# Query and key norms made before the softmax steps, in a one-core MLA, pooling and PEER decoder step

## The reference, cut to what matters

```python
def rmsnorm(x, g):
    y = x * lax.rsqrt(jnp.mean(x * x, axis=-1, keepdims=True) + EPS)
    return y * g
...
q = (cq @ w_uq).reshape(b, t, N_HEADS, QK_NOPE_DIM + QK_ROPE_DIM)
qn = rmsnorm(q[..., :QK_NOPE_DIM], g_qn_nope)
qr = apply_rope(rmsnorm(q[..., QK_NOPE_DIM:], g_qn_rope), cos, sin)
kn = rmsnorm(einsum('...c,chd->...hd', lat, w_uk), g_kn_nope)
s = (einsum('bqhd,bkhd->bhqk', qn, kn) + einsum('bqhr,bkr->bhqk', qr, kr)) * ATTN_SCALE
s = where(k_pos <= q_pos, s, -inf)
p = softmax(s, axis=-1)
ctx = einsum('bhqk,bkc->bqhc', p, lat);  o = einsum('bqhc,chv->bqhv', ctx, w_uv)
```

## Time and profile before

| | us |
|---|---|
| median of 3 runs | 3472.05 (3469.83 to 3478.44) |
| the profiled execution | 3475.48 |
| its span in the trace | 3473.7 |
| attention of tile 0, first score matmul to output projection | 220.68 to 249.08 |
| the same of tile 1 | 297.51 to 329.75 |
| the same of tile 2 | 363.59 to 399.79 |
| PEER gathers | from 478.01 to the end |

### The profile page before, as it was taken

The page is one execution under the profiler, slowest core; times in us unless marked ns, Lnnn a source line. Parts: engine busy times, 40 slices in busy tenths (PEclk is TensorE's granted clock), DMA queues, the critical chain, the costliest instruction groups (busy, mean ns, idle before and its releaser), DMA issues.

```text
span 3473.7 us, 39504 instructions
## 1 busy us (share of the span) xinstructions
PE 2771.9 (80%) x11255; PEld 1237.1 (36%) x11255; DVE 2278.1 (66%) x6380; ACT 1041.5 (30%) x4438; POOL 1221.4 (35%) x1077
## 2 busy tenths in 40 slices
PE   6888889969889957988989769979875676566765
PEld 2344554424434413434434234434331232112321
DVE  2544568887777856777777575777776545565455
ACT  1222224424334412433434324434321111111111
POOL 0000014434333423433434334433444444544343
PEclk8979999989999979999989989999988777777777
DMA  8740059999999989999999999999999999999998
GB/s 329 277 175 34 13 199 408 405 363 404 365 378 413 405 341 371 415 398 406 411 391 403 415 365 405 413 409 410 397 400 410 421 421 408 420 394 369 422 419 358
DMA packets 201396, 1264.74 MB, mean 364 GB/s; under 512 B 23689, under 2 KB 44730, under 8 KB 61393
## 3 DMA queue, kind: packets, MB, share of 16 engines
q0 software_dynamic: 150784, 1091.03, 77.0%
q1 hardware_dynamic: 50393, 171.18, 12.9%
HBM read 1258.79 MB, written 3.79 MB: 363 GB/s over the span
## 4 chain that ended last, share of the span: by engine, by line
PE 41%; DMA 29%; DVE 15%; issue 8%; ACT 3%; POOL 3%; SPq 2%; DVEq 0%; POOLq 0%; ACTq 0%; PEldq 0%
PE bank L1144 14%; DMA ring<-in_uv,work 11%; DMA big<-in_uv,work 7%; PE bank L882 7%; DMA mod_mix<-in_uv,work 7%; PE bank L994 5%; DVE ring L2020 2%; PE bank L899 2%; DMA ring<-in_w_ada 2%; PE bank L828 2%; PE bank L696 1%; ACT work L1473 1%; POOL ring L1512 1%; PE bank L634 1%; PE bank L726 1%
## 5 line engine op out<-in xcount | busy, mean ns | idle before, releaser
L1144 PE MATMUL bank<-ring,work 128*64 128x512 f32 (+1 forms) x2080 | 898.0, 706 | 278.6 <-ACT work L1473 278.4
L1512 POOL DMA_INDIRECT ring<-in_uv,work x520 | 605.2, 1164 | 943.6 <-PE bank L1144 818.4
L2020 DVE CUSTOM_DVE_ANT_0 ring<-ring,mod_smp 128x1024 f32<-128x1024 f32 x512 | 621.9, 1224 | 271.8 <-DMA ring<-in_uv,work 264.7
L1461 ACT ACTIVATE work<-work 128x2 f32<-128x2 f32 x520 | 105.1, 202 | 1494.6 <-DVE work L2020 1494.0
L1512 POOL DMA_INDIRECT big<-in_uv,work x260 | 311.2, 1197 | 686.2 <-PE bank L1144 365.0
L882 PE MATMUL bank<-big 128*128 128x512 f32 x1024 | 515.5, 627 | 0.0
L1144 PE MATMUL bank<-big,work 128*64 128x512 f32 (+1 forms) x1040 | 313.8, 722 | 156.1 <-ACT work L1473 156.0
L1144 PEld LDWEIGHTS bank<-ring,work 128*64 128x64 f32 (+1 forms) x2080 | 207.9, 152 | 625.8 <-ACT work L1473 389.9
L2020 DVE CUSTOM_DVE_ANT_0 big<-big,mod_smp 128x1024 f32<-128x1024 f32 x256 | 309.5, 1224 | 132.4 <-DMA big<-in_uv,work 128.4
L1144 PE MATMUL bank<-work 128*64 128x512 f32 (+1 forms) x520 | 291.2, 688 | 96.2 <-ACT work L1473 96.0
L1473 ACT ACTIVATE work<-small,work 128x64 f32<-128x64 f32 (+1 forms) x1040 | 303.2, 339 | 144.6 <-DVE work L2030 139.0
(11 more groups left out here) (299 smaller groups left out, 3427.7 us busy)
## 6 DMA issues: line engine op xcount, KB each, us to landing
big<-in_wk SPq DMA_DIRECT2D x48, 1152.0 KB, 10.4
ring<-in_w_ada SPq DMA_DIRECT2D x64, 768.0 KB
work<-in_cache_mla SPq DMA_DIRECT2D x104, 160.0 KB, 5.3
ring<-in_uv,work POOLq DMA_INDIRECT x520, 11.8
big<-in_uv,work POOLq DMA_INDIRECT x260, 11.9
ring<-in_w_mla_out SPq DMA_DIRECT2D x1, 4096.0 KB, 14.1
big<-in_w_mla_out SPq DMA_DIRECT2D x4, 1024.0 KB, 11.6
mod_smp<-in_cache_mla SPq DMA_DIRECT2D x24, 160.0 KB, 10.6
```

Source lines behind the costliest of these rows:

```text
L1144: last = mm(out, diag[:, t % 2, j, 0:min(m, HALF)], s[:, D + half * 512:D + (half + 1) * 512], start=(k == 0 and (n < S0 or j == 0)), stop ...
L1461: act.activation(acts[:, t % 2 * GRP:(t % 2 + 1) * GRP], dots[:, t % 2 * GRP:(t % 2 + 1) * GRP], ACT.Gelu)\
L1512: pool.indirect_dma_start(slot[g % SLOTS], None, T["uv"].rearrange("l e d -> (l e) d"), bass.IndirectOffsetOnAxis(index[:, k * GRP + j:k * ...
L2020: dve.tensor_tensor_reduce(u, u, hb, 1.0, 0.0, ALU.mult, ALU.add, dots[:, at:at + 1]).then_inc(sem("dots_set"), 1)
```

## The change

Two edits. First, in `attend` of tiles 0 and 1 the parts 0, 1 and 2 of the next tile's `heads_norm` are executed ahead of the first row max, and the parts 3, 4 and 5 after heads 0, 2 and 4 in place of the parts 0 to 5 after heads 0 to 5. In tile 2 the parts stay where they were. Second, the multiplication of the plain queries by `gqn` (L1621) is kept for the sample tile alone. For the prompt tiles the weight is applied by ACT when it copies the transposed queries out of PSUM: there a query dimension is a partition, so `gqn` becomes a scale operand with one number per partition. That column, `q_gain`, is made once, by multiplying the identity with `gqn` and summing each row.

```diff
+        HEAD_PARTS, HEAD_STEP = (3, 3, 0), (2, 2, 1)
+        q_gain = tiny[:, 50:51]
...
                 for b in range(2):
-                    copy(qnT[:, b * 512:(b + 1) * 512], pb[(4 if i == 1 else 6) + b][:, :])
+                    w.done(act.activation(qnT[:, b * 512:(b + 1) * 512], pb[(4 if i == 1 else 6) + b][:, :], ACT.Copy, scale=q_gain))
...
                 elif part == 3:
                     d(tt(q3[:, :, 0:NOPE], q3[:, :, 0:NOPE], heads(8, NOPE), ALU.mult))
-                    d(tt(q3[:, :, 0:NOPE], q3[:, :, 0:NOPE], over_heads(gqn, NOPE), ALU.mult))
+                    if t == NT:
+                        d(tt(q3[:, :, 0:NOPE], q3[:, :, 0:NOPE], over_heads(gqn, NOPE), ALU.mult))
...
+                if t < NT - 1:
+                    for part in range(HEAD_PARTS[t]):
+                        heads_norm(t + 2, part)
                 row_max(0)
                 row_max(1)
...
                     if h < 6:
                         if t < NT - 1:
-                            heads_norm(t + 2, h)
+                            if h % HEAD_STEP[t] == 0 and HEAD_PARTS[t] + h // HEAD_STEP[t] < 6:
+                                heads_norm(t + 2, HEAD_PARTS[t] + h // HEAD_STEP[t])
...
             d(ts(gqr, gqr, SCALE, None, ALU.mult))
+            d(stt(sq[:, 0:NOPE], ident, 1.0, gqn, ALU.mult, ALU.mult, accum_out=q_gain))
```

## The result

| | before | after |
|---|---|---|
| median of the runs, us | 3474.32 (3466.25 to 3479.07, 8 runs) | 3454.59 (3449.88 to 3462.52, 8 runs) |
| ratio after / before | | 0.995, 95% interval 0.9938 to 0.9962 |
| span of the profiled execution | 3473.7 | 3450.9 |

The interval of the ratio is a gain of 13 to 22 us; the medians differ by 19.7. The forecast was a gain of 17.6 us, to 3454.5.

A forecast was written before the change was run, and what follows sets the result against it. The prediction took DVE to set the length of attentions 0 and 1. Gains of 8.6, 7.8 and 1.2 us in attentions 0, 1 and 2 sum to 17.6, taking 3472.05 to 3454.5 us; range 3446 to 3464.

The forecast's parts named there:

- DVE sets the length: Attentions 0 and 1: DVE decides their length, busy 24.4 of 28.4 and 27.1 of 32.2 us, after idling before each.
- The moved parts are hidden: Parts 0 to 2, 9.1 us per tile, fit DVE's idle time, ending 26 and 6 us before the first row max.
- Attention 0, 8.6 us: Attention 0 gets 8.6 us shorter, taken between 10.0 at full clock and 6.9 at the lower; projection change counted zero.
- The walk with two clocks: Attention 0's sequence rebuilt from row durations: projection starts 10.0 us earlier at full clock, 6.9 at the lower one.
- Attention 1, 7.8 us: Attention 1 gets 7.8 us shorter, taken between 9.7 at full clock and 4.5 at the lower.
- Attention 2, 1.2 us: Attention 2 loses only L1621, 1.26 us; taken as 1.2 us shorter, between 0 and 2.
- No price for the edits: Scaled copies on ACT and making `q_gain` on DVE cost nothing; upper ends 1.2 us per tile and 0.5 us.
- The output weights' cover of 4.6 us: Output weights land at 234.5, first projection wants them at 239 to 240: 4.6 us of cover left from 14.6.
- Full clock: Rival: PE keeps 2.4 GHz through both attentions, gain 23 us, 3449 us; chance 0.13.
- Low clock: Rival: lower clock comes as early as before and lasts into the projection, gain 11 to 12.6 us, 3460; chance 0.17.
- Given back: Rival: the PEER stage keeps 8 us or more of the 17.6 gained, 3463 to 3470 us; chance 0.09.
- Slower: Rival: PEER stage's granted clock drops from 0.93 to 0.91, costing 29 us, 3484 us; chance 0.04.

The follow-up runs named there:

- e2: Changed kernel with the norm weight put back on DVE, so only the parts of the norms move; 3453.97 us, ratio 0.9941.
- e3: Changed kernel with all six parts of the norms ahead of the first row max in tiles 0 and 1; 3444.97 us, ratio 0.9918.
- e4: Changed kernel plus matmuls that nothing reads on PE where it waits for part 4, in attentions 0 and 1; 3454.66 us, ratio 0.9948.
- e1: Changed kernel with all parts put back after heads 0 to 5, so only the scaled copies stay; 3468.31 us, ratio 0.9988.
- e5: e3 with the output weights loaded in two 2 MB halves, each with its own semaphore; 3440.96 us, ratio 0.9897.
- e6: e5 with parts 4 and 5 of the norms in tile 2 moved behind the last softmax step; 3435.83 us, ratio 0.988.
- e7: Changed kernel with parts 3, 4 and 5 after heads 0, 1 and 2 instead of 0, 2 and 4; 3452.47 us, ratio 0.9932.

## Why the prediction was right

- *DVE sets the length.* Right, and shown: e2 and e3 take DVE work out of attentions 0 and 1 and change nothing else, and these shrink.
- *The moved parts are hidden.* Right: 9.0 us from 183.7 and again from 271.45, the second 6.04 us before the first row max; the forecast was 9.1 and 6.
- *Attention 0, 8.6 us.* It measured 7.94, and 0.7 to 0.85 more in the projection behind it, for which I had counted nothing. That the two together meet 8.6 is luck: the term was 0.7 too high, the projection's 0.7 too low. The walk with two clocks gave 10.0 and 6.9. The fall came at part 4's gap, as expected: about 12 us after the first scores, where it came about 8 us after them before.
- *Attention 1, 7.8 us.* This term was mis-sized: 6.3. I put it near the full-clock end (9.7), though the gap was forecast and is followed by the low clock to the end of the attention. e4, without the gap, takes 9.0. The projection behind it was 0.5 shorter, which I had not counted either.
- *Attention 2, 1.2 us.* It measured 1.0 in one profile and 2.5 in the other; e2, where L1621 stays, took 35.85, e1, where it goes, 35.87. The single instruction can't be read from this attention, whose length depends on when the clock falls.
- *The sum.* 17.6 forecast, 16.4 measured up to the first gather. The rest of the difference of the medians, 19.7, lies within the spread of the runs. That the median after, 3454.59, is the forecast to 0.1 us is luck: the kernel before has a median of 3474.32 over eight runs, 2.3 us above the 3472.05 of the three runs that the forecast started from, and 17.6 from that is 3456.7.
- *No price for the edits.* Right within the path. The scaled copy of 128x512 takes 0.69 us, the unscaled one 0.60, so two per tile cost 0.18 us more, well below the 1.2 that was the upper end. The making of `q_gain` went into idle time: DVE's wait behind it is 2.01 us, where it was 2.50. ACT still idles 3.62 us behind the last copy:

```profile
249.87 0.69 ACT L1262 ACTIVATE work<-bank,tiny 128x512 f32<-128x512 f32 x1
250.59 1.22 ACT L1172 ACTIVATE work<-bank 64x512 f32<-64x512 f32 x2
255.43 0.79 ACT L1172 ACTIVATE work<-bank 128x384 f32<-128x384 f32 x2 [3.62 <-PE bank L720]
```

- *The output weights' cover of 4.6 us.* It held here with room: issued at 216.53, they landed 14.0 us later, at 230.5, and the projection started at 237.27, so 6.7 us were left. It is what broke in e3, where attention 0 got 6.6 us shorter still.
- *The rivals.* Full clock: not here. The clock stood at 1.00 over both attentions only in e5 and e6, where all parts were moved. Low clock: partly, it explains the missing 1.5 us of attention 1. Given back: the PEER stage took 2993.2 and 2992.3 us after, 2995.7 and 2997.2 before. Over all profiles it varies by 11.6 us, so these four can't exclude a few us; the medians, with 19.7, leave no room for the 8 us or more of that rival. Slower: the granted clock from 600 to 2500 us was 0.93 after as before, and that rival didn't come about.

## What to carry to other kernels

When an engine is full in one stage and idle just before it, look at what its work there waits for: here part of it could be done in idle time with no other change, and each us moved gave about 0.7 (13.2 of 18.1 in e2). Before such a move, put down when every other input of the next step lands; the first one to become late was a 4 MB load whose issue stood behind an unrelated store. Measure the stretch between two events that follow each other by semaphores rather than the whole time, but cut it into its pieces before you trust a difference: the sums repeated to 0.02 us where the runs spread over 10, and yet the pieces of one kernel differed by 1.5 us and more, and the matmul blocks between the attentions by up to 3 us from profile to profile.

## What the runs showed of the hardware

The clock fell behind much shorter gaps than the 3 us that I had gone by, and not each time. In e7 it fell around a gap of 1.12 us in attention 0. The rows are PE's timeline and two windows of 1 us:

```profile
225.30 0.34 PE L799 MATMUL bank<-small,hT 128*128 128x128 f32 x1 [1.12 <-DVE hT L1759]
```

```profile
225.00:226.00 1.00, 0.70 (x3) 0.66 (x4) 0.90 (x4) 0.27 (x1) 0.00 (x0) 0.74 1.03 426
226.00:227.00 1.00, 1.00 (x6) 0.83 (x4) 0.97 (x2) 0.47 (x3) 0.00 (x0) 0.50 1.00 410
```

The changed kernel has the same gap of 1.12 us at the same place, and its clock stood at 1.00 until part 4. So whether a short gap costs the clock differs between kernels that do the same up to there, which is a spread that no walk through the timeline can foresee. It differs between two executions of one kernel as well. Behind the gap of 1.27 us that follows attention 2, the block of 32 matmuls took 7.14 us in the first profile of the changed kernel and 8.83 in the second, whose clock stood at 0.50 in the first full window of it. In order, the first and the second profile, then that window of the second:

```profile
400.47 7.14 PE L996 MATMUL bank<-big 128*128 128x256 f32 x32 [1.27 <-ACT big L1347]
```

```profile
399.27 8.83 PE L996 MATMUL bank<-big 128*128 128x256 f32 x32 [1.27 <-ACT big L1347]
```

```profile
400.00:402.00 2.00, 2.00 (x6) 1.60 (x5) 0.00 (x0) 0.00 (x0) 0.00 (x0) 0.50 0.00 0
```

In the first profile of the changed kernel the clock, once low in attention 1, stayed low from about 300.5 to 310 us, with PE busy in all of the last 8 us of it.
